# Second layer's attention: the softmax weights are scaled on GpSimd in place of VectorE

## The reference

```python
gates = sigmoid(gl)                                    # per token, head and branch
p_c = softmax(compressed scores); o_c = p_c @ vc       # 15 compressed keys
p_s = softmax(selected scores);   o_s = p_s @ v_sel    # blocks of 64 keys
p_w = softmax(window scores);     o_w = p_w @ v_w      # window of 512 keys
o = gt[..., 0:1] * o_c + gt[..., 1:2] * o_s + gt[..., 2:3] * o_w
```

## Time and profile before

| | us |
|---|---|
| median of 3 runs | 1316.1 |
| lowest and highest run | 1313.63, 1321.33 |
| the profiled execution's own time | 1314.97 |
| its span in the profile | 1312.9 |
| TensorE busy | 1211.2 |
| VectorE busy | 496.1 |
| ScalarE busy | 275.1 |
| GpSimd busy | 113.8 |

### The profile page before, as it was taken

One profiled execution on the slowest core, in us unless ns is written; L12 is line 12 of the kernel. 1 busy time (PEld: TensorE's weight loads), 2 busy tenths in 40 slices (PEclk: granted clock), 3 DMA queues, 4 the chain that ended last, 5 costly groups with the idle time before them and its releaser, 6 DMA issues.

```text
span 1312.9 us, 18617 instructions
## 1 busy us (share of the span) xinstructions
PE 1211.2 (92%) x7752; PEld 702.3 (53%) x7752; DVE 496.1 (38%) x1210; ACT 275.1 (21%) x651; POOL 113.8 (9%) x202
## 2 busy tenths in 40 slices
PE   4899989999799899899987999999999699999996
PEld 4788655434687665643446845655544443332333
DVE  1655542113764773411153643331132640201134
ACT  0113421212112462211122121113320211020110
POOL 2110010000111000100000000000000222122121
PEclk8999999999899899899998999999999799999999
DMA  9977949999946563599996333294325489999993
GB/s 354 386 215 244 386 149 356 387 387 387 338 137 218 200 227 138 197 383 387 387 386 243 136 128 122 73 388 143 105 100 209 174 315 409 393 387 397 386 386 148
DMA packets 173805, 357.46 MB, mean 272 GB/s; under 512 B 15845, under 2 KB 20502, under 8 KB 173718
## 3 DMA queue, kind: packets, MB, share of 16 engines
q1 hardware_dynamic: 171710, 353.14, 73.6%
q10 hardware_dynamic: 2008, 3.07, 0.7%
HBM read 355.14 MB, written 1.05 MB: 271 GB/s over the span
## 4 chain that ended last, share of the span: by engine, by line
PE 60%; DVE 5%; DMA 5%; ACT 3%; issue 1%; SPq 0%; POOL 0%; DVEq 0%; ACTq 0%
PE bank L2775 9%; PE bank L2285 7%; PE bank L3071 4%; PE bank L2424 4%; PE bank L2302 4%; PE bank L2549 4%; DMA ring<-in_w_down 3%; PE bank L3131 3%; PE bank L2349 2%; PE bank L2851 2%; PE bank L2598 2%; DMA ring<-in_moe_w_down 1%; PE bank L2519 1%; PE bank L2717 1%; PE bank L2416 1%
## 5 line engine op out<-in xcount | busy, mean ns | idle before, releaser
L2775 PE MATMUL bank<-ring,A 128*64 128x512 f32 x512 | 115.2, 597 | 1.7 <-DVE pb L1884 1.7
L2549 PE MATMUL bank<-ring,A 128*64 128x512 f32 x512 | 116.0, 598 | 0.0
L2285 PE MATMUL bank<-ring,OT 128*128 128x512 f32 x224 | 97.2, 593 | 1.3 <-ACT OT L1292 0.8
L2349 PE MATMUL bank<-ring,cact 128*32 128x128 f32 x2304 | 85.6, 305 | 9.9 <-DMA ring<-in_ada_w 7.5
L841 POOL TENSOR_TENSOR rstd<-rstd,nhalf 128x1 f32<-128x1 f32 x20 | 15.7, 787 | 796.6 <-DVE rstd L1416 796.5
L2349 PEld LDWEIGHTS bank<-ring,cact 128*32 128x32 f32 x2304 | 70.7, 123 | 24.0 <-issue 15.6
L2775 PEld LDWEIGHTS bank<-ring,A 128*64 128x64 f32 x512 | 34.8, 136 | 71.7 <-issue 70.8
L2285 PEld LDWEIGHTS bank<-ring,OT 128*128 128x128 f32 x224 | 42.2, 190 | 53.5 <-issue 52.5
L2549 PEld LDWEIGHTS bank<-ring,A 128*64 128x64 f32 x512 | 34.3, 136 | 65.3 <-issue 64.2
L2302 PE MATMUL bank<-ring,hT 128*128 128x256 f32 x264 | 62.6, 392 | 2.3 <-ACT hT L966 2.3
L2598 PE MATMUL bank<-ring,pb 128*64 128x512 f32 x256 | 57.7, 597 | 0.2
(11 more groups left out here) (503 smaller groups left out, 1895.4 us busy)
## 6 DMA issues: line engine op xcount, KB each, us to landing
ring<-in_ada_w SPq DMA_DIRECT2D x24, 2048.0 KB, 9.3
ring<-in_moe_w_gate SPq DMA_DIRECT2D x32, 1024.0 KB, 12.3
ring<-in_moe_w_up SPq DMA_DIRECT2D x32, 1024.0 KB, 14.2
ring<-in_moe_w_down SPq DMA_DIRECT2D x16, 2048.0 KB, 19.8
ring<-in_w_gate SPq DMA_DIRECT2D x16, 2048.0 KB, 11.2
ring<-in_w_up SPq DMA_DIRECT2D x16, 2048.0 KB, 11.2
ring<-in_w_down SPq DMA_DIRECT2D x16, 2048.0 KB, 20.4
ring<-in_w_in SPq DMA_DIRECT2D x13, 2048.0 KB, 19.6
```

Of the source, the lines that this page charges most:

```text
L2285: ins = mm(B[2 * (m % 2) + tt][:], lhs[:, c, tt * P:(tt + 1) * P], w[:, c, :], start=c == 0, stop=c == C - 1)
L2349: ins = mm(B[MOD_RAW_BANK[G]][32 * q:32 * (q + 1), k * P:(k + 1) * P], cact[:, c0 + c:c0 + c + 1].broadcast_to([P, 32]), w[:, c, q * P:(q ...
L2549: ins = mm(B[b][64 * odd:64 * (odd + 1), :], wide_h[c][:, slot:slot + 64], w[:, 2 * pair + odd, :, r, :], start=c == 0, stop=c == C - 1)
L2775: ins = mm(B[b][64 * odd:64 * (odd + 1), :], wide_h[c][:, slot:slot + 64], w[:, 2 * pair + odd, r, :], start=c == 0, stop=c == C - 1)
```

## The change

GpSimd gets a new function `weights_scaled("att1")` between its last rotation and the next norm's power. For each softmax item it waits for the exponentials, raises the sums to the power -1, multiplies by the gates, and multiplies the weights in four pieces (one for each head and each half of the tokens) by one scalar per partition. VectorE no longer scales in `att1`. The transposes of `att1` wait for a new semaphore `p_scaled`; `p_ready` now counts the items of `att0` and `att2` alone, which `scaled_on_dve` turns into the right value.

```diff
+    minus_one = sb("minus_one", [P, 4])
...
+    def scaled_on_dve(u):
+
+        return u + 1 if u < SOFT["att1"] else u + 1 - (SOFT["att2"] - SOFT["att1"])
...
+        g.memset(minus_one[:], -1.0)
...
+        def weights_scaled(name):
+
+            items = [it for it in ITEMS[name] if it["soft"] is not None]
+            for n, it in enumerate(items):
+                u, b = it["soft"], SCORE_OF[it["soft"]]
+                h, branch = it["gate"]
+                pool.wait_ge(s["exp_done"], u + 1)
+                step(g.tensor_tensor(rr[:, b], rs[:, b], minus_one[:].rearrange("p (a i) -> p a i", i=2), ALU.pow))
+                step(g.tensor_tensor(rr[:, b], rr[:, b], gts[:, :, 3 * h + branch:3 * h + branch + 4:3], ALU.mult))
+                for q in range(2):
+                    sl = slice(0, P) if q == 0 else slice(P, 384)
+                    for i in range(2):
+                        ins = g.tensor_scalar(score[b][:, i, sl], score[b][:, i, sl], rr[:, b, q, i:i + 1], None,
+                                              ALU.mult)
+                ins.then_inc(s["p_scaled"], 1)
...
+        weights_scaled("att1")
...
-                if 0 <= t - 1 < len(items) and items[t - 1]["soft"] is not None:
+                if name != "att1" and 0 <= t - 1 < len(items) and items[t - 1]["soft"] is not None:
...
-                    if it["gate"] is not None:
-                        h, branch = it["gate"]
-                        step(v.tensor_tensor(rr[:, b], rr[:, b], gts[:, :, 3 * h + branch:3 * h + branch + 4:3],
-                                             ALU.mult))
...
-                            pe.wait_ge(s["p_ready"], it["soft"] + 1)
+                            if name == "att1":
+                                pe.wait_ge(s["p_scaled"], it["soft"] - SOFT[name] + 1)
+                            else:
+                                pe.wait_ge(s["p_ready"], scaled_on_dve(it["soft"]))
```

## The result

The changed kernel takes 1329.65 us (median of 4 runs, 1327.64 to 1330.28) against 1317.03 us for the kernel before (4 runs, 1313.63 to 1321.33). The medians differ by 12.6 us; the ratio on record, which is used from here on and need not equal the quotient of two medians, is 1.0084 with a 95% interval of [1.0059, 1.0109]: slower by 0.8%, some 11 us, outside the forecast range of 1312 to 1322. One execution of a later kernel (before_cmp_on_vector), of 1823.31 us at a granted clock of 0.65, is left out of its ratio. The profiled execution has a span of 1328.5 us, 15.6 more than before.

What follows compares the result with a forecast made beforehand. TensorE was taken to set the pace. Start +0.1 us net, middle and end nothing: 1316.1 + 0.1 = 1316.2 us, range 1312 to 1322.

Steps and rivals of the forecast that it cites:

- Four multiplications by one scalar per partition: GpSimd's scaling of one unit's weights, two of 128 columns and two of 256: 1.4 us, bounds 1.2 and 2.36.
- room of 4.0 us: Second layer's attention: time for scaling each unit, between the end of its exponentials and its transposes on TensorE.
- loop of 4.88 + L: Transposes, next scores, exponentials, GpSimd's step, transposes: 4.88 + L against the 8.88 us period, deciding from L = 4.0 on.
- L: Length of GpSimd's step for one unit, from exponentials to TensorE's transposes: 2.89 us, bounds 2.1 and 4.7.
- power: GpSimd raising one unit's sums, 128x4, to the power -1: 1.02 us, bounds 0.55 and 1.66.
- product: GpSimd's product of the 128x4 factors with the gates: 0.19 us, bounds 0.10 and 0.45.
- waits: Two waits between dependent steps on GpSimd within one unit: 0.08 us each.
- hand-over to TensorE: End of GpSimd's step, passing the scaled unit to TensorE: 0.03 us, an estimate.
- rival 1: GpSimd's step is longer than the room: at L = 4.7 some +9 us, 1325; chance 0.08.
- Rival 2: VectorE's maxima and GpSimd's step disturb each other through the mask in SBUF: 1319 us; chance 0.08.
- Rival 3: Relief of VectorE pays more than counted: all of the 1.4 us of waits goes, 1314.7 us; chance 0.10.
- the gaps are ScalarE's: TensorE's gaps in the stage: 3.5 us in eight pieces wait for ScalarE's copy of the compressed branch, unchanged.

Runs made afterwards that it cites:

- before_cmp_on_vector: The kernel before, with both copies to PT of a compressed item on VectorE instead of one each on VectorE and ScalarE; 1315.39 us, ratio 0.9982.
- the run with single prices: The kernel before, with GpSimd running single instructions on scratch data in its idle time, two samples of each; one execution, 1313.49 us.
- two_tensor: The changed kernel with GpSimd's four multiplications replaced by two products of two tensors, the factors broadcast; 1315.97 us, ratio 0.9988 to before.
- no_product: The changed kernel with GpSimd's multiplication cut to one column, so the weights go unscaled; 1316.88 us, ratio 0.9983 to before.
- factor_only: The changed kernel with GpSimd making only power and gate product, VectorE multiplying the weights after waiting for it; 1316.02 us, ratio 0.9999 to before.
- lag3: The changed kernel with LAG of att1 at 3 instead of 2, each unit transposed one step later; 1321.22 us, ratio 1.0028 to before.
- product_only: The changed kernel with VectorE making reciprocal and gate product, GpSimd only the four multiplications; 1325.59 us, ratio 1.0063 to before.
- two_tensor_long: two_tensor with a second power and a small product on spare columns ahead of each unit, for the changed kernel's step length; 1329.48 us, ratio 1.0080 to before.

## Why the prediction was wrong

**The step that failed** is one term of the sum: "Four multiplications by one scalar per partition ... 2 x (0.29 + 0.40) = 1.38, taken as 1.4". They measure 2.98 us. The select and the copy were taken as their neighbours because they too have one full input; the run with single prices shows a slope 2.5 times that of the copy or more. Its upper bound of 2.36, "as if two-input", was no bound either: the product of two tensors is the cheaper form (1.61 us for the same data, in two instructions). That form was in the kernel before, on VectorE; the prediction did not set the two forms against each other.

**The frame held.** The room of 4.0 us, the loop of 4.88 + L and the decision at L = 4.0 were read rightly: with the step inside the room two_tensor, no_product and factor_only lie within 0.2% of before and lag3 within 0.3%, those beyond it are slower by 0.6 and 0.8%, and a kernel stretched across the line with other instructions reproduces the loss. The other terms of L came out: power 1.04 for 1.02, product 0.20 for 0.19, waits 0.08 and 0.10 for 0.08 and 0.08. The hand-over to TensorE measures 0.15 for 0.03. L is 4.63, inside the stated bounds of 2.1 to 4.7, at their upper end.

**What happened is rival 1**, to which I gave 0.08. Its reason, that it "takes nearly every upper bound at once", was false: one term alone, far over its bound, was enough. Its price of +9 us at L = 4.7 was low. In the profile the stage loses 10.9 us by the step: 3.2 at the first two units (3.4 in the rival), 5.6 in six periods (5 for seven), 2.1 at the last (1). The loop formula gives 9.5 us for the period, the measured mean is 9.85, since in every other period the second unit of a pair also queues behind the first. TensorE's clock, which I had not counted, adds 2.8 us behind the last unit. The 1.74 us of the compressed scores belong to neither. This split rests on one profile of each kernel.

**Rival 2** (the maxima disturbed) is refuted: they stay at 0.29 and 0.42 us, with GpSimd at work beside them. **Rival 3** (relief of VectorE) won nothing that can be told in no_product and factor_only. But the prediction's sentence that the gaps are ScalarE's and that "nothing in that chain gets shorter" holds only while the copy stays on ScalarE. The relief and the move of that copy together were worth 0.4%. The move alone gave 0.2%, which can't be told from nothing; in the middle of the stage the two profiles show 1.0 us for the move alone and 3.0 for both.

## What to carry to other kernels

Work taken off an engine that nobody waits for is worth nothing until something that is waited for takes its place; work put on another engine must fit the room between its input and the first who needs it, and that room can be read off the timeline before anything is built. Price an operation by rows of the very same form (operation, kind of second operand, width), and where there is none, let the upper bound go well past its neighbours: here one full input and a scalar cost nearly twice what two tensors, one of them broadcast, cost. When work moves to another engine, move it first in the form that it has. When the length against a limit decides, give the far side a chance by the worst-known term, not by the count of terms.

## What the runs showed of the hardware that was not expected

- GpSimd's multiplication by a scalar from SBUF takes 0.30 us at 4 columns, 0.61 at 128 and 0.92 at 256; its product of two tensors, one broadcast, 0.61 at 256 columns and 1.04 at 512. Per unit that is 2.98 against 1.61 us.
- GpSimd's power grows by about 0.16 us for each column: 0.55 at one, 0.70 at two, 1.01 to 1.04 at four, 1.66 at eight.
- TensorE's clock can fall again soon after it has risen. The three kernels whose step does not fit (changed, product_only, two_tensor_long) have their longest wait, 2.49, 3.03 and 2.76 us, just before the stage's first transposes (443.14, 444.98 and 444.95). Their granted clock is 0.63, 0.56 and 0.59 in the window from 444, after 0.93, 0.87 and 0.83 in the window before. The other kernels, whose waits there are 1.26 us at most, stay at 1.00 once they are back at it, until 532.
- The same three show a fall between 516 and 524 (0.50, 0.57, 0.55 at the lowest), and here the long waits do not explain it. Only in the changed kernel does it follow one (2.03 us until 517.09). In product_only it follows waits of 0.57 and 0.61 us, and the products that start at 516.04 take 1.50 us in place of 0.87; in two_tensor_long the products at 515.90 take 1.08 us before its wait of 1.75 us has begun. What makes the clock fall was not tested and stays open, and so does whether a wait can cost more than its own length in this way.
